# The recurrence's forget inputs and queries by crossed 512-column products, with the weights' splits moved ahead of the queries' sigmoids

## The reference

```python
h = _rmsnorm(x, norm_mix_g[l])
z = h @ w_in[l]
(hq, hf, hi, hg, fq, fk, fv, ff, mq, gate_logits) = jnp.split(z, pts, axis=-1)
# the recurrence:
f = lb + (1.0 - lb) * jax.nn.sigmoid(f_logit)        # f_logit = hf
qh = heads(jax.nn.silu(q))                           # q = hq
kh = heads(1.0 - f)
G = jnp.cumsum(heads(jnp.log(f)), axis=3)
# then products q_t k_s exp(G_t - G_s) between positions t and s
```

## Time and profile before

| | us |
|---|---|
| median of 3 runs (947.80 to 947.99) | 947.92 |
| the profiled execution | 948.22 |
| its span, first to last instruction | 946.4 |

### The profile page before, as it was taken

How to read it: one execution, slowest core, us unless ns; L and a number is a source line. 1 busy time by engine, 2 the same in 40 slices (tenths; PEclk the granted TensorE clock), 3 DMA queues, 4 the chain that set the end, 5 groups by cost and what they waited for, 6 DMA issues and landing times.

```text
span 946.4 us, 13932 instructions
## 1 busy us (share of the span) xinstructions
PE 939.1 (99%) x5616; PEld 810.4 (86%) x5616; DVE 686.3 (73%) x985; ACT 518.8 (55%) x657; POOL 76.0 (8%) x149
## 2 busy tenths in 40 slices
PE   9999999999999999999999999999999999999997
PEld 9988887788888888888888888889898888888886
DVE  6788667877868777788876757578678677576675
ACT  6776766555356556555655445356546465354554
POOL 1010228171100000000000000000002000000000
PEclk9999999999999999999999999999999999999999
DMA  9844555343565454556364555654534446646451
GB/s 355 333 157 161 175 185 216 134 151 132 187 246 180 172 196 169 220 178 222 137 233 165 198 203 178 222 178 138 201 128 159 156 140 217 222 148 224 162 178 45
DMA packets 26112, 175.11 MB, mean 185 GB/s; under 512 B 3256, under 2 KB 3520, under 8 KB 6080
## 3 DMA queue, kind: packets, MB, share of 16 engines
q1 hardware_dynamic: 25168, 170.15, 50.6%
q10 hardware_dynamic: 880, 4.07, 1.2%
HBM read 173.15 MB, written 1.06 MB: 184 GB/s over the span
## 4 chain that ended last, share of the span: by engine, by line
PE 98%; DMA 1%; DVE 0%; ACT 0%; SPq 0%; issue 0%; ACTq 0%
PE ps L410 52%; PE ps L417 25%; PE ps L421 13%; PE ps L523 1%; PE ps L753 1%; PE ps L769 1%; DMA FP<-in_first 1%; PE ps L804 1%; PE ps L622 1%; PE ps L674 1%; PE ps L818 0%; PE ps L734 0%; PE ps L784 0%; PE ps L541 0%; PE ps L701 0%; PE ps L853 0%
## 5 line engine op out<-in xcount | busy, mean ns | idle before, releaser
L1574 DVE TENSOR_TENSOR Wl<-raw,Wh 128x2048 fp32r<-128x2048 f32 x151 | 345.9, 2293 | 38.0 <-ACT Wh L1083 37.4
L1083 ACT ACTIVATE Wh<-raw 128x2048 fp32r<-128x2048 f32 x154 | 294.3, 1913 | 38.2 <-PE ps L410 34.0
L417 PE MATMUL ps<-hT,Wh 128*128 128x512 f32 x1056 | 247.9, 390 | 0.0
L417 PEld LDWEIGHTS ps<-hT,Wh 128*128 128x128 f32 x1056 | 197.1, 188 | 40.2 <-issue 0.2
L410 PE MATMUL ps<-Wh,hT 128*128 128x512 f32 (+1 forms) x640 | 200.8, 386 | 0.0
L410 PEld LDWEIGHTS ps<-Wh,hT 128*128 128x128 f32 x640 | 118.3, 188 | 24.5 <-issue 1.9
L1417 ACT ACTIVATE Am<-ps 128x512 f32<-128x512 f32 x66 | 39.1, 593 | 178.5 <-PE ps L421 176.3
L421 PEld LDWEIGHTS ps<-hT,Wl 128*128 128x128 f32 x1056 | 132.4, 192 | 3.4
L421 PE MATMUL ps<-hT,Wl 128*128 128x256 f32 x1056 | 133.4, 283 | 0.0
L1659 DVE TENSOR_TENSOR PT<-ps,Am 128x256 f32<-128x256 f32 x132 | 49.7, 418 | 108.1 <-ACT Am L1417 107.9
L410 PE MATMUL ps<-Wh,yTh 128*128 128x512 f32 (+1 forms) x314 | 123.1, 392 | 0.0
(11 more groups left out here) (248 smaller groups left out, 805.4 us busy)
## 6 DMA issues: line engine op xcount, KB each, us to landing
raw<-in_units SPq DMA_DIRECT2D x154, 1024.0 KB, 4.8
FP<-in_bias ACTq DMA_DIRECT2D x1, 2048.0 KB, 11.3
FP<-in_first SPq DMA_DIRECT2D x2, 768.0 KB, 8.3
FP<-in_first SPq DMA_DIRECT2D x3, 384.0 KB, 4.9
raw<-in_units SPq DMA_DIRECT2D x2, 512.0 KB, 10.8
X<-in_x SPq DMA_DIRECT2D x1, 1024.0 KB, 17.4
Hn<-in_mem SPq DMA_DIRECT2D x1, 1024.0 KB, 9.0
XT<-in_mem_turned SPq DMA_DIRECT2D x1, 1024.0 KB, 11.0
```

The costliest lines, as they stand in the source:

```text
L417: pe.matmul(o, lh(k), hT_both(k), start=first and k == ks[0], stop=False)
L1083: act.activation(wh[j % NS][:, 0:n], raw[j % NR][:, 0:n], ACT.Copy).then_inc(w_hi, 1)
L1574: dve.tensor_tensor(wl[j % NS][:, 0:n], raw[j % NR][:, 0:n], wh[j % NS][:, 0:n].bitcast(F32), ALU.subtract).then_inc(w_lo, 1)
```

## The change

1. hf and hq go by `wide` and `narrow` (a new `crossed_rows`; hf's unit 0 written out, its first half starting on half a unit). Each block m has a bank of its own: eight banks' worth in place of four, all taken from T.
2. ACT copies each of these eight banks to SBUF (`keep_front`, into G, Vm, Iv and K, not yet in use then). DVE adds the two halves of each unit (`front_joined`) and multiplies with RB (`front_made`): `front_rows`, two operations a unit in place of one.
3. The lower bounds are made around the norm, ahead of hq's second low part; their Exp on ACT moves ahead of the first Sigmoid.
4. DVE's four multiplies for f go ahead of the queries. For the queries DVE splits hi's second unit, joins, scales and multiplies hq's first; splits the first gate's first unit, joins, scales and multiplies hq's second. ACT's high parts of these units go likewise ahead of the two sigmoids.
5. The sum `lams` comes last, behind the queries' second multiply; lambda's Exp on ACT follows the queries' second sigmoid.

```diff
+            def crossed_rows(key, banks, mid=None):
+                i = U[key]
+                for m in range(2):
+                    b = banks.take()
+                    t = take(key + (m,), b)
+                    if m == 0:
+                        pe.wait_ge(w_hi, i + 1)
+                    wide(t, weight_left(i, 256, m * 128)[0], EIGHT, True)
+                    if m == 0:
+                        weights(i)
+                    narrow(t, weight_left(i, 256, m * 128)[1], EIGHT, True).then_inc(ps_full[b], 1)
+                    if m == 0 and mid:
+                        mid()
+                unit_end[i] = full(key + (1,))
...
-            rows_out(("hf", 1), T)
-            rows_out(("hq", 0), T, mid=lambda: spread(0))
-            rows_out(("hq", 1), WF)
+            crossed_rows(("hf", 1), T)
+            crossed_rows(("hq", 0), T, mid=lambda: spread(0))
+            crossed_rows(("hq", 1), T)
...
+            def keep_front(key, m):
+                act.wait_ge(*full(key + (m,)))
+                act.activation(front_kept(key)[:, m * 512:m * 512 + 512], bank[at[key + (m,)][0]][:, :],
+                               ACT.Copy).then_inc(*emptied(key + (m,)))
...
             hi_to(U["hq", 0])
+            keep_front(("hf", 0), 0)
             act.wait_ge(x_in, 16)
             squares(0, 1)
             squares(0, 0)
+            keep_front(("hf", 0), 1)
+            act.wait_ge(lb_sub, 2)
+            act.activation(lbe, lbe, ACT.Exp).then_inc(lb_exp, 1)
+            keep_front(("hf", 1), 0)
             hi_to(U["hq", 1])
...
+            keep_front(("hf", 1), 1)
             hi_to(U["hi", 0])
+            keep_front(("hq", 0), 0)
...
-            for u in range(2):
-                begin(("hq", u))
-                act.wait_ge(*free(("hq", u)))
-                act.activation(E1[:, u * 512:u * 512 + 512], Q[:, u * 512:u * 512 + 512], ACT.Sigmoid).then_inc(q_sig, 1)
-            act.wait_ge(lb_sub, 2)
-            act.activation(lbe, lbe, ACT.Exp).then_inc(lb_exp, 1)
+            keep_front(("hq", 0), 1)
+            begin(("hq", 1))
+            keep_front(("hq", 1), 0)
+            act.wait_ge(front_made, 3)
+            act.activation(E1[:, 0:512], Q[:, 0:512], ACT.Sigmoid).then_inc(q_sig, 1)
+            keep_front(("hq", 1), 1)
+            begin(("hi", 0))
+            act.wait_ge(front_made, 4)
+            act.activation(E1[:, 512:1024], Q[:, 512:1024], ACT.Sigmoid).then_inc(q_sig, 1)
             act.wait_ge(lam_sum, 1)
             act.activation(lams, lams, ACT.Exp).then_inc(lam_exp, 1)
...
+            def front_rows(dst, key):
+                n, d, r = FRONT.index(key), v3(dst), front_kept(key)[:, :].rearrange("p (m s n) -> p m s n", m=2, s=2)
+                for m in range(2):
+                    dve.wait_ge(*free(key + (m,)))
+                dve.tensor_tensor(d, r[:, :, 0, :], r[:, :, 1, :], ALU.add).then_inc(front_joined, 1)
+                dve.wait_ge(front_joined, n + 1)
+                dve.tensor_tensor(d, d, by_token(2), ALU.mult).then_inc(front_made, 1)
+                dve.wait_ge(front_made, n + 1)
...
+            lo_to(U["hq", 1])
+            spread_out(0)
+            for u in range(2):
+                front_rows(E0[:, u * 512:u * 512 + 512], ("hf", u))
+            lo_to(U["hi", 0])
...
-            dve.wait_ge(lam_mul, 2)
-            dve.tensor_reduce(lams, lamp.rearrange("p (a b) -> p a b", a=2), AXX, ALU.add).then_inc(lam_sum, 1)
-            dve.wait_ge(*seq.now())
             for h in range(4):
 ...
+            for u in range(2):
+                lo_to(U["hi", 1] + u)
+                s = Q[:, u * 512:u * 512 + 512]
+                front_rows(s, ("hq", u))
+                dve.wait_ge(q_sig, u + 1)
+                dve.tensor_tensor(s, s, E1[:, u * 512:u * 512 + 512], ALU.mult).then_inc(q_made, 1)
+            dve.wait_ge(lam_mul, 2)
+            dve.tensor_reduce(lams, lamp.rearrange("p (a b) -> p a b", a=2), AXX, ALU.add).then_inc(lam_sum, 1)
             begin(("hi", 0))
             dve.wait_ge(lg_neg, 1)
```

More of the change, by code:

```diff
@@ L193, in build @@
         ff_hi, ff_lo, x0_hi = sem("ff_hi"), sem("ff_lo"), sem("x0_hi")
+        front_joined, front_made = sem("front_joined"), sem("front_made")
         xt_hi, xt_lo, mt_hi, mt_lo = (sem(n) for n in ("xt_hi", "xt_lo", "mt_hi", "mt_lo"))
@@ L349, in crossed_out, with front_kept @@
             return Am[:, n % 2 * 512:n % 2 * 512 + 512]
+        FRONT = (("hf", 0), ("hf", 1), ("hq", 0), ("hq", 1))
+        def front_kept(key):
+            return (G, Vm, Iv, K)[FRONT.index(key)]
         def yT_at(k):
@@ L639, in pe_program @@
             unit_end[U["hg", 0]] = unit_end[U["hg", 1]] = full(("hg", 1, 1))
-            i, b = U["hf", 0], T.take()
-            t = take(("hf", 0), b)
+            i = U["hf", 0]
             for m in range(2):
+                b = T.take()
+                t = take(("hf", 0, m), b)
+                wh_m, wl_m = weight_left(i, 256, m * 128)
+                for n, ks in enumerate((EIGHT[0:4], EIGHT[4:8])):
+                    if m == 0:
+                        pe.wait_ge(*((w_hi, i + 1) if n else (w1_hi, 1)))
+                    wide(t, wh_m, ks, n == 0)
                 for n, ks in enumerate((EIGHT[0:4], EIGHT[4:8])):
@@ L645, in pe_program @@
                         pe.wait_ge(*((w_lo, i + 1) if n else (w1_lo, 1)))
-                    ins = three(t[:, m * 256:m * 256 + 256], weight_left(i, 256, m * 128), right(hT_at), ks, n == 0, n == 1)
-            ins.then_inc(ps_full[b], 1)
-            unit_end[i] = full(("hf", 0))
-            rows_out(("hf", 1), T)
-            rows_out(("hq", 0), T, mid=lambda: spread(0))
-            rows_out(("hq", 1), WF)
+                    ins = narrow(t, wl_m, ks, n == 1)
+                ins.then_inc(ps_full[b], 1)
+            unit_end[i] = full(("hf", 0, 1))
+            crossed_rows(("hf", 1), T)
+            crossed_rows(("hq", 0), T, mid=lambda: spread(0))
+            crossed_rows(("hq", 1), T)
             WF.n = 6
@@ L1173, in act_program @@
                 s = E0[:, u * 512:u * 512 + 512]
-                act.wait_ge(*free(("hf", u)))
+                act.wait_ge(front_made, u + 1)
                 act.activation(s, s, ACT.Sigmoid).then_inc(f_sig, 1)
-            for u in range(2):
-                begin(("hq", u))
-                act.wait_ge(*free(("hq", u)))
-                act.activation(E1[:, u * 512:u * 512 + 512], Q[:, u * 512:u * 512 + 512], ACT.Sigmoid).then_inc(q_sig, 1)
-            act.wait_ge(lb_sub, 2)
-            act.activation(lbe, lbe, ACT.Exp).then_inc(lb_exp, 1)
+            keep_front(("hq", 0), 1)
[7 more added lines that the diff above has]
+            act.activation(E1[:, 512:1024], Q[:, 512:1024], ACT.Sigmoid).then_inc(q_sig, 1)
             act.wait_ge(lam_sum, 1)
@@ L1699, in dve_program @@
             lo_to(U["hq", 0])
[L1700 to L1716, removed]
             L0, L1 = VT[:, ROWS["lb"]:ROWS["lb"] + 4], VT[:, ROWS["lb"] + 4:ROWS["lb"] + 8]
@@ L1722, in dve_program @@
             dve.tensor_tensor(lbe[:, 4:8], L1, lbm, ALU.subtract).then_inc(lb_sub, 1)
+            dve.wait_ge(c_in, 16)
+            norm_end(0)
             dve.wait_ge(lb_exp, 1)
@@ L1730, in dve_program @@
             dve.tensor_scalar(omlb, lb, -1.0, 1.0, ALU.mult, ALU.add).then_inc(*seq.next())
-            dve.wait_ge(lam_mul, 2)
-            dve.tensor_reduce(lams, lamp.rearrange("p (a b) -> p a b", a=2), AXX, ALU.add).then_inc(lam_sum, 1)
-            dve.wait_ge(*seq.now())
+            lo_to(U["hq", 1])
[3 more added lines that the diff above has]
+            lo_to(U["hi", 0])
+            for m in range(2):
+                s = Sg[:, m * 512:m * 512 + 512]
+                dve.wait_ge(g_sig, m + 1)
+                dve.tensor_tensor(s, s, P[m][:, :], ALU.mult).then_inc(g_made, 1)
             for h in range(4):
```

## The result

| | kernel before | changed kernel |
|---|---|---|
| median, us (21 runs each) | 948.07 (947.76 to 948.66) | 949.44 (948.77 to 949.82) |
| the profiled execution | 948.22 | 949.56 |
| its span | 946.4 | 947.7 |

The ratio is 1.0013, 95% interval 1.0007 to 1.0019: the changed kernel is 1.4 us slower. The interval lies above 1, so the loss is there, but it is within the 0.2% that count as no change here. The forecast was 949.4.

The account below looks back on a forecast made before the run. TensorE was taken as the bound, without slack: gain -0.81, waits +0.9 and +1.35 make +1.45 us, 949.7 against the profiled 948.22, 949.4 for the median. This case alone 948.9 to 949.9; the range takes in 947.0 and 950.8.

Parts of the forecast that it names:

- What bounds the kernel: Whole span: TensorE, busy 99%, waits for nothing from hf on, so every wait put on it is paid in full.
- TensorE's gain: hf and hq: 64 triples at 0.360 us become pairs at 0.347, a gain of 0.81 us.
- The chain up to the low part: VectorE's steps from hq's second low part to that of the gate's second unit, forecast from 55.7 to 57.95.
- The first wait: First gate's second unit: TensorE wants its low part at 57.04, ready at 57.95, a new wait of 0.9 us.
- the sum: First level's start at 65.0 instead of 63.54: -0.81 + 0.9 + 1.35 = +1.45 us; without waits, gate's second unit at 57.04.
- The second wait: First level: decays end at 64.95, TensorE held up by 0.9 wants them at 63.6, a wait of 1.35 us.
- step 2: VectorE copies RB at 31.8, TensorE's spread coming 0.5 earlier; two multiplies then become four operations, 2.9 us, to 35.1.
- ScalarE's eight copies: Bank copies of about 0.51 us back to back; the first three go where ScalarE idles, no bank is late.
- No waits: Rival: TensorE's two new waits don't arise, the gain alone is left, 947.1; chance 0.17.
- The early Exp's table: Rival: lower bounds' Exp needs another table load, 1.3 us ahead of hq's second high part; +2.4, 950.3; chance 0.18.
- The clock: Rival: two waits of 0.9 and 1.4 us might drop TensorE to 1.2 GHz; 951 to 953; chance 0.05.
- Weight loads as the bound: Rival: weight loads bound hf and hq, a third less gives up to 7.8 us: 941; chance 0.02.

## Why the prediction was right

Its steps, by what the runs showed:

- **What bounds the kernel.** Right: TensorE's waits alone decide. The difference of the spans, 1.3, is the delay of the first level, 1.31, and levels behind it don't wait.
- **TensorE's gain.** The mechanism was right, the size 0.14 too large: 0.67 for 0.81. In the feed-forward 32 matmuls of a kind follow one another; here 8 wide take 19.33 - 17.49 = 1.84, 0.230 each and not 0.2275, so each change between the forms adds some 0.02 us. It is still four times the 0.16 that the prediction worked out, as an estimate, from the fixed cost per matmul that the Trainium skill gives ("TensorE: Matmul & The Clock Gate", "Wait — 56ns, not 53.3ns?"); this trace does not agree with it.
- **The chain up to the low part.** Forecast 55.7 to 57.95, measured 55.56 to 57.84. The single steps hold as well: hi's second low part at 40.18 (40.1), the gate's first at 46.77 (46.7), lambda's Exp done at 52.57 (52.5), `lg_neg` at 54.09 (54.25). That they hold so well is in part luck. RB was copied at 32.10 and not at 31.8, since TensorE's spread came only 0.19 earlier than before; f's four multiplies took 1.30 for 1.54 and GpSimd's five operations 1.44 for 1.7, which took it back.
- **The first wait.** Forecast 0.9, measured 0.41. Most of that is TensorE's: it began hf 0.24 later, by hg's wait, gained 0.14 less, and so came to this unit 0.44 later than the 57.04 of the sum, at 57.48. VectorE was 0.11 early.
- **The second wait.** Forecast 1.35, measured 1.23, with the decays at 64.80 for 64.95. The first level starts when VectorE is ready, and what TensorE gains or loses behind its spread only changes how long it waits. So most of the 0.81 in the sum had no weight in the result; its place is in the two waits. What TensorE loses ahead of the spread does count, because VectorE's copy of RB waits for it: in the kernel with lambda early hf starts 0.25 earlier, RB is copied 0.24 earlier (31.86 for 32.10), and the gate's first low part begins 0.20 earlier (46.57 for 46.77). The prediction uses this link only for its gain of 0.5 (step 2). In the profiled execution hg's wait went through it, so of the 1.31 that agree with the sum's 1.45 the change itself made 1.07.
- **ScalarE's eight copies.** Right: the first three lie ahead of the raw data's landing, and none of the banks was late.
- **The rivals.** No waits: it was not so, but the kernel with lambda and one high part moved shows how near it was. The early Exp's table: none was loaded, and the price put on it was too high. The prediction had 0.2 of it under ScalarE's wait and 0.1 under VectorE's; the run with two tables shows 0.9 taken up, so that one table of 1.3 would have put the first level back by some 0.4, as an estimate, and not by 0.95. The clock: it held at the waits of 0.4 and 1.2 (granted clock 1.00 from 56 to 70); a single one of 2.7 brought it down. Weight loads as the bound: with a third of them fewer the stage is 0.67 shorter, not 7.8.

## What to carry to other kernels

Where the engine that bounds a kernel has no waits, an edit that gives it less to do is worth that much only as long as its suppliers stay ahead; read the lead of each supplier at each deadline (3.2 and 1.9 us here) and add to its path every operation and every stand in another engine's queue, before counting the gain. Look for a trifle in the chain: here two sums and their exponentials for lambda, moved behind the queries, held a third engine, and with it the weights' low part, for 2 us. An engine's idle time in front of a late step (3.7 us of ScalarE's) is where the step behind it can go.

## What was not expected

- One wait of 2.68 us of TensorE, within a dense stretch, was followed by a granted clock of 0.50 and cost 2.9 us more in the profiled execution, doubling its price; waits of 0.71, 1.44 and 1.19 us with matmuls between them left it at 1.00 in theirs. What lies between these cases was not tried.
- A path over two engines shortens by the smaller of their gains: without the joins VectorE was free for hi's second low part 1.3 us earlier and waited 1.27 of it for ScalarE. And what one execution's loads do can be as large as what an experiment is to show: 0.24 us by a piece for hg in the changed kernel, 0.77 by a weight unit in the kernel without joins. So the starts ahead of the change have to be compared before a difference behind it is read.
